# ScalarE begins the second block's convolution and squares, VectorE makes all low parts, GpSimd none

## The reference, cut to what matters

```python
for l in range(2):
    h = rmsnorm(x, norm1) * (1 + sc1) + sh1
    q, k, v, g, alr, z, xs, bm, cm, dt = split(h @ w_in)
    log_a = log_sigmoid(alr @ gla_a_w + gla_a_b) / 16       # summed in chunks of 64 tokens
    o = rmsnorm(gla_chunked(q, k, v, log_a)) * silu(g)
    xs, bm, cm = split(silu(causal_conv4([xs, bm, cm]) + conv_b))
    dt = softplus(dt + dt_bias)
    y = ssd_chunked(xs, dt, -exp(a_log), bm, cm) + d_skip * xs
    y = rmsnorm(y * silu(z))
    x = x + g1 * ([o, y] @ w_out)
    h = rmsnorm(x, norm2) * (1 + sc2) + sh2
    x = x + g2 * (swiglu(h) if l == 0 else moe_swiglu(h))   # 8 experts, each 1024 x 3584, top 2
return rmsnorm(x, final_norm)
```

## Time and profile before

| | |
|---|---|
| median of 3 runs (lowest, highest) | 2893.75 us (2886.74, 2896.32) |
| the profiled execution | 2894.8 us |
| its span | 2893.0 us |
| granted TensorE clock, mean | 0.971 |
| TensorE, VectorE, ScalarE, GpSimd busy | 2802.2, 2025.8, 1680.4, 554.8 us |
| mixer 0, routing, experts | from about 1274, 1848, 1864 us |

### The profile page before, as it was taken

One profiled execution on the slowest core, in us unless ns is written; L12 is line 12 of the kernel. 1 busy time (PEld: TensorE's weight loads), 2 busy tenths in 40 slices (PEclk: granted clock), 3 DMA queues, 4 the chain that ended last, 5 costly groups with the idle time before them and its releaser, 6 DMA issues.

```text
span 2893.0 us, 43985 instructions
## 1 busy us (share of the span) xinstructions
PE 2802.2 (97%) x19002; PEld 2633.4 (91%) x19002; DVE 2025.8 (70%) x1997; ACT 1680.4 (58%) x1821; POOL 554.8 (19%) x230
## 2 busy tenths in 40 slices
PE   8999999999999999998999998999999999999998
PEld 7999999999999999987999998899888988988897
DVE  5677647766676557758477756587877877787785
ACT  4555446554554455543477633576767776676774
POOL 1000000001000000024000024143433433343342
PEclk9999999999999999988999997899999999999998
DMA  7545456726445467522588732499999999999995
GB/s 243 164 145 175 146 191 235 263 84 180 150 133 176 145 233 253 190 85 88 199 292 292 248 93 73 162 375 342 359 337 357 346 346 358 341 363 337 355 347 189
DMA packets 356313, 679.18 MB, mean 235 GB/s; under 512 B 17264, under 2 KB 238736, under 8 KB 355984
## 3 DMA queue, kind: packets, MB, share of 16 engines
q1 hardware_dynamic: 340800, 617.54, 61.3%
q0 software_dynamic: 15312, 58.75, 6.2%
HBM read 675.19 MB, written 4.69 MB: 235 GB/s over the span
## 4 chain that ended last, share of the span: by engine, by line
PE 79%; DVE 12%; ACT 6%; issue 2%; DMA 1%; SPq 0%; ACTq 0%; DVEq 0%
PE bank L596 76%; DVE w_lo L1393 4%; ACT w_hi L2013 3%; DVE ring_tail L1352 1%; PE bank L676 1%; PE bank L1200 1%; ACT ring_tail L2082 1%; DVE ring_tail L1354 1%; PE bank L701 1%; DVE gates L1406 1%; PE bank L636 1%; DVE ring_low L1315 0%; PE bank L727 0%; DVE probs L1720 0%; DMA ring_head<-in_w_in 0%
## 5 line engine op out<-in xcount | busy, mean ns | idle before, releaser
L1906 DVE TENSOR_TENSOR ew_lo<-ring_head,ew_hi 128x1792 fp32r<-128x1792 f32 (+1 forms) x288 | 682.4, 2402 | 196.4 <-ACT ew_hi L2356 196.4
L2356 ACT CAST ew_hi<-ring_head 128x1792 fp32r<-128x1792 f32 (+2 forms) x384 | 647.3, 1693 | 275.9 <-PE bank L596 275.8
L581 POOL TENSOR_TENSOR ew_lo<-ring_head,ew_hi 128x1792 fp32r<-128x1792 f32 (+1 forms) x96 | 388.3, 4045 | 669.2 <-ACT ew_hi L2356 669.2
L596 PE MATMUL bank<-xs_hi,ring_low 128*128 128x256 f32 (+1 forms) x2608 | 510.6, 282 | 0.0
L596 PEld LDWEIGHTS bank<-xs_hi,ring_low 128*128 128x128 f32 (+1 forms) x2608 | 412.8, 189 | 1.2 <-issue 0.3
L1393 DVE TENSOR_TENSOR w_lo<-ring_head,w_hi 128x2048 fp32r<-128x2048 f32 x108 | 247.5, 2291 | 131.5 <-ACT w_hi L2013 131.5
L596 PE MATMUL bank<-x_hi,w_hi 128*128 128x256 f32 x1152 | 323.3, 286 | 15.1 <-DVE w_lo L1393 14.7
L596 PE MATMUL bank<-x_hi,w_lo 128*128 128x256 f32 x1152 | 318.5, 283 | 0.0
L596 PE MATMUL bank<-x_lo,w_hi 128*128 128x256 f32 x1152 | 318.4, 283 | 0.0
L596 PE MATMUL bank<-ew_hi,xe_hi 128*128 128x448 f32 x1024 | 294.2, 368 | 1.4 <-DVE ew_lo L1906 1.4
L596 PE MATMUL bank<-ew_lo,xe_hi 128*128 128x448 f32 x1024 | 290.8, 365 | 0.0
(11 more groups left out here) (422 smaller groups left out, 5924.5 us busy)
## 6 DMA issues: line engine op xcount, KB each, us to landing
ring_head<-in_moe_w_gate SPq DMA_DIRECT2D x128, 896.0 KB, 6.6
ring_head<-in_moe_w_up SPq DMA_DIRECT2D x128, 896.0 KB, 7.0
ring_head<-in_moe_w_down SPq DMA_DIRECT2D x96, 1024.0 KB, 7.2
ring_head<-in_w_in SPq DMA_DIRECT2D x82, 1024.0 KB, 5.3
ring_tail<-in_ada_w POOLq DMA_DIRECT2D x48, 1024.0 KB, 7.3
ring_head<-in_ffn_w_in SPq DMA_DIRECT2D x44, 1024.0 KB, 6.2
ring_head<-in_ffn_w_out SPq DMA_DIRECT2D x22, 1024.0 KB, 7.7
ring_head<-in_xa_kv SPq DMA_DIRECT2D x16, 1024.0 KB, 5.3
```

The source lines that it names most:

```text
L581: pool.tensor_tensor(ew_lo[:, h, 0:n], ring(c % 6)[:, 0:n], ew_hi[:, h, 0:n].bitcast(F32), ALU.subtract).then_inc(w_used[c % 6], 1)
L596: ins = nc.tensor.matmul(out, lhsT, rhs, start=start, stop=stop, **kw)
L1906: v.tensor_tensor(ew_lo[:, h, 0:n], ring(c % 6)[:, 0:n], ew_hi[:, h, 0:n].bitcast(F32), ALU.subtract).then_inc(w_used[c % 6], 1)
L2356: a.copy(ew_hi[:, c % DEPTH_HI, 0:n], ring(c % 6)[:, 0:n]).then_inc(f.count(part_hi), 1)
```

## The change

Three things change in the mixers. ScalarE copies banks 0 to 2 and does tap 3 of the convolution from them (`conv_first`), VectorE the other taps bank by bank. alr gets a row of ones and its weight the bias as 17th row, and both are multiplied turned round, directly behind the transposes; the decay's sums over 64 tokens are four products with a block of the causal mask on bank 4 in place of the scans, and the factor 1/16 goes into the exponentials. o is copied and squared by ScalarE. GpSimd does no low part any more, in mixers or experts; VectorE does all of them. Ten idle products on bank 1 are put into routing. The parameters come by seven DMAs, not five. The steps of 896 columns are as before.

```diff
-POOL_LOW = range(3, 14)
...
+                pool.dma_start(kb[16:17, 2 + l, :], io["gla_a_b_2"][l]).then_inc(par2_in, 16)
...
-                pool.tensor_tensor(ring_low[:, at, 0:n], ring(at)[:, 0:n], high[:, 0:n].bitcast(F32), ALU.subtract).then_inc(chunk_lo, 1)
-            for i in POOL_LOW:
-                mixer_low(0, i)
...
-            for i in POOL_LOW:
-                mixer_low(1, i)
...
-                        if c % 4 == 3:
-                            pool.wait_ge(part_hi, f.now(part_hi))
-                            pool.tensor_tensor(ew_lo[:, h, 0:n], ring(c % 6)[:, 0:n], ew_hi[:, h, 0:n].bitcast(F32),
-                                               ALU.subtract).then_inc(w_used[c % 6], 1)
-
...
-            def idle_products(n):
+            def idle_products(n, b=7):
 
                 for _ in range(n):
-                    nc.tensor.matmul(bank[7][:, :], zeros[:, 0:P], zeros[:, :], start=True, stop=True)
+                    nc.tensor.matmul(bank[b][:, :], zeros[:, 0:P], zeros[:, :], start=True, stop=True)
 
...
-                three(1, 5, xs, mixer=True)
-
                 open_bank(2)
-                for j in range(2):
-                    mm(bank[2][:, j * TOK:(j + 1) * TOK], kb[0:16, 2 + l, j * P:(j + 1) * P], alr[0:16, :], True, True,
-                       bank_full[2] if j else None)
-                three(6, 6, xs, turned=True, mixer=True)
-
+                for t in range(2):
+                    mm(bank[2][:, t * TOK:(t + 1) * TOK], alr[0:17, t * P:(t + 1) * P], kb[0:17, 2 + l, :], True, True,
+                       bank_full[2] if t else None)
                 if l:
                     modulation(4, range(36, 48), 24, True)
+                three(1, 5, xs, mixer=True)
                 pe.wait_ge(dta_ready, f.next(dta_ready))
...
+                pe.wait_ge(decay_out, f.next(decay_out))
+                open_bank(4)
+                if l:
+                    pe.wait_ge(mods_taken, 5)
+                for j in range(2):
+                    for t in range(2):
+                        mm(bank[4][:, j * TOK + t * P:j * TOK + (t + 1) * P], zt[:, t, j * P:(j + 1) * P], const[:, C_DIAG:C_DIAG + P],
+                           True, True, bank_full[4] if j and t else None)
+                three(6, 6, xs, turned=True, mixer=True)
...
-                if l:
-                    pe.wait_ge(mods_taken, 5)
...
-                pe.wait_ge(normed_sq, f.next(normed_sq))
+                taken(0)
+                taken(1)
...
+                    idle_products(6, 1)
...
+                    idle_products(4, 1)
...
-            dve.wait_ge(par2_in, f.next(par2_in, 80))
+            dve.wait_ge(par2_in, f.next(par2_in, 112))
...
-                for c, dst in enumerate([hc[:, 0:2, :], hc[:, 2:4, :], kb[:, 0:2, :]]):
-                    take(c, dst)
-
-                dve.wait_ge(f.last, f.now(f.last))
+                v.memset(att, 0.0).then_inc(f.count(vector_step), 1)
                 raw = [hc[:, j, :] for j in range(4)] + [kb[:, j, :] for j in range(2)]
                 dst = [qb[:, j, :] for j in range(4)] + [ka[:, j, :] for j in range(2)]
-                for tap in (3, 2, 1, 0):
-                    s = 3 - tap
-                    for j in range(6):
-                        w = p2[:, B_CW + 6 * tap + j:B_CW + 6 * tap + j + 1]
-                        if s == 0:
-                            ins = v.tensor_scalar(dst[j], raw[j], w, p2[:, B_CB + j:B_CB + j + 1], ALU.mult, ALU.add)
-                        else:
-                            ins = v.scalar_tensor_tensor(dst[j][:, s:TOK], raw[j][:, 0:TOK - s], w, dst[j][:, s:TOK], ALU.mult, ALU.add)
-                    ins.then_inc(f.count(conv_in if tap == 0 else vector_step), 1)
-                    if tap == 3:
-
-                        dve.wait_ge(bank_full[3], f.next(bank_full[3]))
-                        v.tensor_copy(alr[0:NARROW, :], bank[3][0:NARROW, 0:TOK]).then_inc(rows_ready, 1)
-                    dve.wait_ge(f.last, f.now(f.last))
+                for c in range(3):
+                    f.bump(bank_full[c])
+                    f.bump(bank_free[c])
+                    dve.wait_ge(conv_raw, f.next(conv_raw))
+                    for tap in (2, 1, 0):
+                        back_by = 3 - tap
+                        for j in (2 * c, 2 * c + 1):
+                            w = p2[:, B_CW + 6 * tap + j:B_CW + 6 * tap + j + 1]
+                            ins = v.scalar_tensor_tensor(dst[j][:, back_by:TOK], raw[j][:, 0:TOK - back_by], w, dst[j][:, back_by:TOK],
+                                                         ALU.mult, ALU.add)
+                        ins.then_inc(f.count(conv_in if (c, tap) == (2, 0) else vector_step), 1)
+                        if tap:
+                            dve.wait_ge(f.last, f.now(f.last))
+                    if c < 2:
+                        mixer_low(l, 3 + c)
+                dve.wait_ge(bank_full[3], f.next(bank_full[3]))
+                v.tensor_scalar(alr[0:NARROW, :], bank[3][0:NARROW, 0:TOK], const[0:NARROW, C_LIVE:C_LIVE + 1], ident[0:NARROW, 16:17],
+                                ALU.mult, ALU.add).then_inc(rows_ready, 1)
+                mixer_low(l, 5)
 
                 dve.wait_ge(bank_full[3], f.next(bank_full[3]))
                 v.tensor_tensor(tiles(dtraw, 2), tiles(bank[3][:, TOK:TOK + 16], 2), spread(p2[:, B_DTB:B_DTB + 8], 2), ALU.add).then_inc(f.count(bank_free[3]), 1)
                 dve.wait_ge(f.last, f.now(f.last))
                 v.scalar_tensor_tensor(dtabs, dtraw, -1.0, dtraw, ALU.mult, ALU.max).then_inc(f.count(dt_in), 1)
-                for c in range(2):
-                    take(c, qa[:, 2 * c:2 * c + 2, :])
-                dve.wait_ge(bank_full[2], f.next(bank_full[2]))
-                z = ka[:, 2:4, :]
+                take(2, zt)
+                dve.wait_ge(f.last, f.now(f.last))
+                v.scalar_tensor_tensor(tiles(scores[:, 0, :], 2), zt, -1.0, zt, ALU.mult, ALU.max).then_inc(f.count(decay_in), 1)
+                take(0, qa[:, 0:2, :])
+                mixer_low(l, 6)
                 if l:
                     mods_take(4, 1, 24, 24, 4)
                     with_bias(1, 5, 24, 48)
-                for j in range(2):
-                    v.tensor_scalar(z[:, j, :], pairs(2)[:, j, :], p2[:, B_AB + j:B_AB + j + 1], None, ALU.add).then_inc(f.count(bank_free[2] if j else vector_step), 1)
-                dve.wait_ge(f.last, f.now(f.last))
-                v.scalar_tensor_tensor(tiles(scores[:, 0, :], 2), z, -1.0, z, ALU.mult, ALU.max).then_inc(f.count(decay_in), 1)
 
...
-                v.scalar_tensor_tensor(z, z, 0.0, tiles(scores[:, 0, :], 2), ALU.min, ALU.subtract).then_inc(f.count(vector_step), 1)
-                dve.wait_ge(f.last, f.now(f.last))
-                v.tensor_scalar(z, z, 1.0 / 16, None, ALU.mult).then_inc(f.count(vector_step), 1)
-                dve.wait_ge(f.last, f.now(f.last))
-                run = probs[:, 0, :].rearrange("p (n c) -> p n c", c=64)
-                zc = z.rearrange("p j (n c) -> p (j n) c", c=64)
-                for n in range(8):
-                    ins = v.tensor_tensor_scan(run[:, n, :], one.to_broadcast([P, 64]), zc[:, n, :], 0.0, ALU.mult, ALU.add)
-                ins.then_inc(f.count(vector_step), 1)
-                dve.wait_ge(f.last, f.now(f.last))
-                v.tensor_tensor(scores[:, 1, :].rearrange("p (n c) -> p n c", c=64), run[:, :, 63:64].broadcast_to([P, 8, 64]), run,
-                                ALU.subtract).then_inc(f.count(cum_ready), 1)
+                v.scalar_tensor_tensor(zt, zt, 0.0, tiles(scores[:, 0, :], 2), ALU.min, ALU.subtract).then_inc(f.count(decay_out), 1)
+                take(1, qa[:, 2:4, :])
+                mixer_low(l, 7)
                 dve.wait_ge(conv_silu, f.next(conv_silu))
...
+                    if q == 2:
+                        run = probs[:, 0, :].rearrange("p (n c) -> p n c", c=64)
+                        take(4, probs[:, 0, :], bank[4])
+                        dve.wait_ge(f.last, f.now(f.last))
+                        v.tensor_tensor(scores[:, 1, :].rearrange("p (n c) -> p n c", c=64), run[:, :, 63:64].broadcast_to([P, 8, 64]), run,
+                                        ALU.subtract).then_inc(f.count(cum_ready), 1)
...
+                mixer_low(l, 8)
...
+                mixer_low(l, 9)
...
+                mixer_low(l, 10)
...
+                mixer_low(l, 12)
...
+                mixer_low(l, 11)
                 for j in range(2):
-                    take(j, merged[:, 2 * j:2 * j + 2, :])
-                dve.wait_ge(f.last, f.now(f.last))
-                v.tensor_tensor(osq, merged[:, 0:4, :], merged[:, 0:4, :], ALU.mult).then_inc(f.count(normed_sq), 1)
+                    f.bump(bank_full[j])
+                    f.bump(bank_free[j])
 
...
+                    if j == 0:
+                        mixer_low(l, 13)
...
-                        if c % 4 == 3:
-                            f.bump(part_hi)
```

(36 more changed lines are left out.)

30 lines of the change are left out of this document (9 added, 21 removed).

## The result

The changed kernel takes 2864.14 us (median of 5 runs, 2852.36 to 2870.06) against 2893.75 of the kernel before, whose runs lie between 2886.74 and 2896.32. The ratio is 0.9897 with a 95% interval of 0.9867 to 0.9927: 30 us faster, between 21 and 38. The prediction said 2878 and a range of 2867 to 2890. The execution that was profiled is the shortest of the five: 2852.36 us, span 2850.6.

The account below looks back on a forecast made before the run. The prediction took TensorE, busy 97% of the span, as the bound, with time to win only where it waits or runs slowly. Its terms summed to -15.6 us from 2893.75, giving 2878, range 2867 to 2890.

Parts of the forecast that it names:

- The waits: Mixers: TensorE's waits for alr, dta, bank 2 and gla_in all go, -24.4 us; +1.0 if one spare time fails.
- The clock: Mixers: slow products behind waits regain full clock, -1.9 in mixer 0, -1.8 in mixer 1; +1.9 for a newly slow chunk.
- The +1.9 for mixer 1's chunk 5: Mixer 1: one-column products now directly ahead make chunk 5 begin at a slow clock, +1.9 us, between 0 and 5.9.
- Bank 4's products: Mixers: four added 128x128 products on bank 4 cost 1.4 us in each mixer, +2.7 in all.
- The DMAs ahead of fin: Two more DMAs in GpSimd's queue ahead of fin's delay VectorE before the standard deviation is inverted, +1.1 us.
- Routing: Idle products delay the gather 2.4, higher clock returns 2.7, a 1.4 wait goes: net -1.0 us, between -2.7 and +1.9.
- The experts: Part 47 in VectorE's queue delays eact_lo 0.8 us at seven experts' ends, 1.2 at the last: +6.8, from 1.2 to 15.
- Rival (a): VectorE becomes the bound of the experts, eact_lo some 5 us late in each of 8: +18, 2911 us; chance 0.06.
- (b): Mixers: waits are exchanged for others at gla_in and bank 6, 12 us come back: 2890 us; chance 0.14.
- (c): Better than counted: boundary wait hidden, mixer 1's chunk 5 keeps the clock, spare times hold: -24.1, 2870 us; chance 0.12.

Follow-up runs that it names:

- stall_alone: The changed kernel with low part 5 ahead of alr's copy and seven memsets between the two, in both mixers, so alr alone is late: 2878.99 us.
- before_idle_in_waits: The kernel before with idle products of zeros in the mixers' waits, nothing ready earlier: 2887.34 us, ratio 0.9982.
- before_experts_vector: The kernel before with the experts' low parts all on VectorE, mixers and routing as before: 2901.90 us, ratio 1.0021.
- eact_first: The changed kernel with eact_lo ahead of low part 47 in VectorE's queue at each expert's end: 2855.54 us, ratio 0.9869.
- mixer_lows_gpsimd: The changed kernel with the mixers' low parts 3 to 13 back on GpSimd: 2886.81 us, ratio 0.9974.
- before_mixer_lows_vector: The kernel before with the mixers' low parts 3 to 13 on VectorE instead of GpSimd: 2871.76 us, ratio 0.9936.
- mods_behind: The changed kernel with mixer 1's last modulation (one-column products) behind chunk 5 instead of ahead of it: 2863.59 us.

## Why the prediction was right and wrong

**The waits** (-24.4, +1.0): right. 24.0 us went, and a wait of 0.24 us at gla_in in each mixer is left, where 1.3 us to spare was forecast; dta came 0.3 us early where 1.5 was forecast. The two spare times were overrated by over a us each, and that neither returned as a long wait was narrow.

**The clock** (-1.9, -1.8, +1.9, together -1.8): this is the step that failed. The mechanism, slow products behind a wait, was in the prediction; its size was not. It charged the fall once in mixer 0, behind alr, and in mixer 1 the excess of 6.36 over 5.45, a price itself at the half clock, and "about as much again". In truth each of the waits for alr, dta, bank 2 and gla_in had slow products behind it. The busy time fell by 13.5 us although the bank 4 products added 1.6; the term was -15.1 and not -1.8. Of this 13.9 us are the half clock by its own record; where the other 1.2 lie is not shown. The rows were in the trace: the granted clock over the two stretches was 0.86 and 0.82, that is up to 20.9 us of the 61.3 and 68.2 busy (an estimate from above, since part of the low clock lies in the waits), against the 3.7 us that the prediction charged. stall_alone shows 2.4 us for one fall, before_idle_in_waits that the same products run fast when TensorE doesn't stand. The +1.9 for mixer 1's chunk 5 was right (2.1 measured). By the page "TensorE: Matmul & The Clock Gate" of the Trainium skill (What's actually happening) half rate is the default and activity releases it. The prediction used that rule for the gather, where it held (3.84 us behind the idle products, 6.50 without), and not for the other places.

**Bank 4's products** (+2.7): 1.6, 0.81 in each mixer from their start to chunk 6. Their price came from the row of 5.45 us, itself at half clock; the same products take 3.82.

**The DMAs ahead of fin** (+1.1): nothing, 0.1 at most. From the last variance product to the first on std it is 1.10 us before and 1.16 after.

**Routing** (-1.0): -3.1, of which 1.7 up to the first expert product and 1.4 the wait for ew_lo behind it. The gather did get the full clock, the best case that the step allowed for, and -3.1 lies beyond its -2.7. before_experts_vector reached the same 91.0 without idle products and with a slow gather, so most of the 1.7 may be luck.

**The experts** (+6.8): right. The stage grew by only 4.0, which holds two gains as well, the 1.4 just named and 1.4 below. The delay is 0.81 per expert where 0.8 was forecast, VectorE is busy 174.6 of 200 us where 174 was, and the difference to eact_first, 7.0, is 7 x 0.81 and 1.3 for the last expert. Rival (a) fell: the mean part is 2.0 us. The page "SBUF — State Buffer" of the Trainium skill (Who interferes with whom) excludes VectorE operations with two SBUF inputs and GpSimd ones that read SBUF from each other. mixer_lows_gpsimd and before_mixer_lows_vector agree with it: six operations take 8.5 us longer beside 9.1 us of GpSimd, and eight scans 10.28 us or 1.57.

**Rivals (b) and (c).** No wait took the place of another. The result is beyond (c), 2870, but not by (c)'s reasons: chunk 5 of mixer 1 did not keep the clock, and the wait at the experts' ends was not hidden. It is the clock term again.

**The sum of the profiled pair**: -24.0 + 1.6 + 0.1 - 15.1 - 3.1 + 6.8 - 1.4 (not forecast) is -35.1, and -7.3 is the untouched first block, together the 42.4 us between the two spans. The -1.4 lie at the end of the program for the most part. From the first expert product on TensorE had the half clock for 15.4 us before and for 11.3 after; before was the unlucky one, since two runs with the same experts, before_mixer_lows_vector and before_idle_in_waits, had 10.9 and 11.4. The median difference, 30, is smaller than 35. The executions that were not profiled can't be divided into stages, so where the other 5 us lie stays open. Their times do go with the mean granted clock, 0.983 for the profiled execution and 0.976 to 0.980 for the other four.

## What to carry to other kernels

A wait of the bounding engine costs its length and the slow clock behind it: add up the busy time that TensorE spends at the half clock over the whole stretch and count half of it, instead of charging single places. Take the price of a new operation from a row at full clock. Two engines that hold each other up aren't relieved by dividing work between them: in the mixers the same low parts were cheaper all on VectorE. In the experts they were so only with the queue in the right order, 1025.7 us in eact_first against 1032.7 in the changed kernel and 1027.5 to 1028.7 in the three traces with the experts of before.

## What was not expected of the hardware

- A fall of the clock costs about the same behind a short wait as behind a long one: chunk 5 took 8.23 us behind waits of 2.1 and 0.6, 8.14 behind 6.9, 7.36 behind 6.6 (where alr's products took part of the fall), against 5.87. Behind waits of 0.24 and 0.31 us the clock stayed at 1.00 in mixer 0.
- The clock fell during products of one column while TensorE was busy without a break, and mixed among products of 256 columns too (0.50 from 1695 on). Where they moved behind chunk 5, the slow products moved with them (mods_behind). How soon it falls differs between executions of one kernel, 4.2 and 1.1 us behind the first of them.
- The eight scans of 64 columns take 1.57 us alone and took 10.28 beside GpSimd's low parts, and a 128x16 operation took 0.18 instead of 2.41.
- An untouched stretch of some 1270 us differs by 14 us between executions. In the shortest TensorE had the half clock for 38 to 41 us of it, in the longest for 65.
